# Output projection's norm and operand split moved into the heads' steps, meta tokens left out of the dense stages

## Chip, cores and metric

One NeuronCore of one Trainium2 chip runs the program. The metric is device time in microseconds, median of the runs shown. TensorE (PE), VectorE (DVE), ScalarE (ACT), GpSimd (POOL) and SyncE (SP, which only issues transfers here) each work through a queue of their own in order, and wait for each other by semaphores.

## What is computed

One layer of a hybrid encoder on T = 1152 token columns: 48 columns of padding, 16 learned meta tokens, 1024 prompt tokens and 64 sample tokens. All dense products are in fp32 accuracy.

```
proj = rms_norm(x, norm1) @ w_in                 # 1024 -> 2560 columns
o_r  = rwkv7_time_mix(proj[..., :1792], ...)     # 8 heads x 64, state recurrence, times the gate g
o_a  = window_attention(q, k, v, ...)            # 8 query heads, 2 kv heads, meta keys and sinks
o_a  = rms_norm(o_a, attn_out_norm)              # over the 512 columns of o_a
h    = x + concat(o_r, o_a) @ w_out              # 1024 -> 1024
u    = rms_norm(h, norm2) @ w_up                 # 1024 -> 4096
y    = h + square(relu(u)) @ w_down              # 4096 -> 1024
```

The outputs are y without the meta tokens, the new recurrent states, the last projected rows, and the attention's window and meta rows.

## The kernel before

Everything is kept with the features on the 128 partitions and the tokens along the row. A dense product splits both operands into an upper part rounded to fp32r and the rest, and adds three fp32r products (`three_pass`, L98 to L102: hi x hi, hi x lo, lo x hi). The tokens of a dense product come in three groups of columns (`GROUPS`, L25): 336, 384 and 384, each with a PSUM bank of its own.

`phase_project` makes the buffer `proj` (20 units of 128 features x 1152 columns): units 0 to 3 are r, 4 to 7 k, 8 to 11 v, 12 and 13 the low-rank inputs, 14 to 17 q, 18 and 19 the attention's k and v.

`phase_heads` (`loop_heads`, L630) goes through nine steps j of 128 tokens. Each engine has its own hand-written order of small functions (`step`), and PSUM banks go from use to use by a written list (`SCHEDULE`, L586; class `Fills` turns it into semaphore counts). A step inverts a 64 x 64 triangular system in five levels: PE multiplies (`product(j, l)`), DVE masks (`product`, L1259, the tile `Pm`), PE multiplies twice (`extend(j, l)`), ACT copies both results (`extended`, the tiles `X` and `XT`). Between the levels lie the attention of step j, the preparation (`prep_...`) of step j+1 and the output (`out_mean`, `out_var`, `out_gate`, `finish`) of step j-1. The attention's result is written over q in `proj` (`attended`, L1081) and the mixer's over r (`finish`, L1298, its last line L1308). On ACT `prep_rn` (L1032) makes the rstd of the keys in two passes, for which `prep_kkn` (L1188) waits on DVE; behind it in DVE's queue is the mask of level 4. POOL's `prep_rk` (L1408) waits for `prep_kkn`'s first line, `normed` (L1461) for ACT's `rstd`.

After the last step a barrier ends the phase (`end_phase`). `phase_block` then runs `mix_heads` (L1507): squares of o_a on ACT, their sums on DVE and through PE, the rstd on ACT, the scaling on DVE (L1558), and the split of all eight units into the new buffers `mix_hi` and `mix_lo`, upper parts on ACT, lower parts on DVE and, for three units of r, on POOL (L1569). Meanwhile SP fetches the first two column blocks of `w_out` (`out_fetch`, L1578, three transfers per block). `project_out` (L1642) then splits each block of `w_out` on ACT (L1684) and DVE (L1700), multiplies, adds x by a product with the identity (L1729), and starts the second norm; `mlp` (L1744) runs 16 blocks of 256 hidden units: `up` (48 matmuls for each of three groups of columns), ACT's relu, square and rounding, DVE's lower part (`hidden`), and `down` (48 per group), which DVE adds to h (`add`, L1918, L1923). In DVE's queue the adds of a block stand behind `up_weights` (L1900), the split of the next weights but one, which in turn waits for ACT's `up_weights` (L1849). A `down` matmul group with index 6 or more waits for the add six before it, since there are six banks.

Of the kernel before, what the change touches and what calls it, by code (L numbers as in the profile page):

```python
# [48 lines left out]
def build_program(nc, i, o):  # L49

    with ExitStack() as whole:
# [31 lines left out]
        def col(name, t=0, n=1):  # L83
# [4 lines left out]
                 w_stage=w_stage, bank=bank, col=col, bias=bias,  # L88
# [6 lines left out]
        phase_block(nc, i, o, s, projected.close)  # L95
# [360 lines left out]
def phase_heads(nc, i, o, s):  # L456
# [3 lines left out]
    with ExitStack() as ctx:  # L460
# [24 lines left out]

        kst = buf("kst", [P, 2, 144])
# [10 lines left out]
class Setup:  # L497
# [72 lines left out]
    def tensor(self, pe):  # L570
# [8 lines left out]
        for p in range(4):  # L579
# [50 lines left out]
def loop_heads(nc, s, v, setup, i, o):  # L630
# [19 lines left out]
        sem(n, 2) for n in "mx_ok nm_ok sk_ok se_ok pexp_ok den_ok rec_ok p_ok".split())  # L650
    hp_t, hp_c, cache_v = (sem(n) for n in "hp_t hp_c cache_v".split())
# [24 lines left out]
    AR = lambda j: AR2[:, j % 2]  # L676
    LAST = NT - 1

    with nc.Block() as block:
        @block.tensor  # L680
        def _(pe):
# [223 lines left out]
            def step(j):  # L905
# [73 lines left out]
            out_mean(LAST)  # L979
            out_var(LAST)  # L980
# [14 lines left out]
        def _(act):  # L995
# [112 lines left out]
            def step(j):  # L1108
# [52 lines left out]
            states = [proj[0:64, 9 + n, 0:512] for n in range(2)]  # L1161
            for n, dst in enumerate(states):
                act.activation(dst, bank[1 - n][0:64, :], ACT.Copy).then_inc(hp_c.sem, 1)
            for n, (src, name) in enumerate(zip(states, ("wkv_p", "wkv_s"))):
                act.wait_ge(hp_c.sem, hp_c.n(n))
                act.dma_start(o[name].rearrange("a b h v k -> v (a b h) k"), src.rearrange("v (h k) -> v h k", h=8)).then_inc(s["wkv_out"].sem, 16)

        @block.vector
        def _(dve):
# [139 lines left out]

            def transfers(j):  # L1310
# [165 lines left out]

# [28 lines left out]


def mix_heads(nc, i, s, v):  # L1507

    sem, proj, eps, bank, col, ones = (s[k] for k in "sem proj eps bank col ones".split())
    x_hi, x_lo = v["x_hi"], v["x_lo"]  # L1510
    s["wo_in"] = [sem(f"wo_loaded{b}", 48) for b in range(2)]
    sq_ok, added, sum_ok, ln_ok, rs_ok, scaled, hi_r, hi_a = (
        sem(f"mix_{n}") for n in "sq added sum ln rs scaled hi_r hi_a".split())

    def heads(t, c=PAD, n=T - PAD):

        return proj[:, t if t < 4 else 10 + t, c:c + n]

    with nc.Block() as block:
        @block.sync  # L1520
        def _(sp):
            for m in range(2):
                out_fetch(sp, i, s, m)
            sp.wait_ge(s["wkv_out"].sem, 32)

        @block.scalar
        def _(act):
            for t in range(4):
                act.activation(proj[:, 4 + t, PAD:T], heads(4 + t), ACT.Square).then_inc(sq_ok.sem, 1)
            for t in range(4):  # L1530
                act.activation(x_hi[:, t, PAD:T], heads(t), ACT.Copy).then_inc(hi_r.sem, 1)
            for g, (c, n) in enumerate(GROUPS):
                rs = proj[:, 8, c:c + n]
                act.wait_ge(sum_ok.sem, sum_ok.n(g))
                act.activation(rs, bank[g][:, 0:n], ACT.Ln, bias=eps[:, 0:1], scale=1.0 / 512).then_inc(ln_ok.sem, 1)
                act.wait_ge(ln_ok.sem, ln_ok.n(g))
                act.activation(rs, rs, ACT.Exp, scale=-0.5).then_inc(rs_ok.sem, 1)
            for g, (c, n) in enumerate(GROUPS):
                for t in range(4):
                    act.wait_ge(scaled.sem, scaled.n(4 * g + t))  # L1540
                    act.activation(x_hi[:, 4 + t, c:c + n], heads(4 + t, c, n), ACT.Copy).then_inc(hi_a.sem, 1)

        @block.vector
        def _(dve):

            for k, t in enumerate((1, 2, 3)):
                dve.wait_ge(sq_ok.sem, sq_ok.n(t))
                if k > 0:
                    dve.wait_ge(added.sem, added.n(k - 1))
                dve.tensor_tensor(proj[:, 4, PAD:T], proj[:, 4, PAD:T], proj[:, 4 + t, PAD:T], ALU.add).then_inc(added.sem, 1)  # L1550
            for t in range(3, 4):
                dve.wait_ge(hi_r.sem, hi_r.n(t))
                dve.tensor_tensor(x_lo[:, t, PAD:T], heads(t), x_hi[:, t, PAD:T].bitcast(F32), ALU.subtract)
            for g, (c, n) in enumerate(GROUPS):
                dve.wait_ge(rs_ok.sem, rs_ok.n(g))
                for t in range(4):
                    a = heads(4 + t, c, n)
                    dve.scalar_tensor_tensor(out=a, in0=a, scalar=col("an", t), in1=proj[:, 8, c:c + n],  # L1558
                                             op0=ALU.mult, op1=ALU.mult).then_inc(scaled.sem, 1)
                for t in range(4):  # L1560
                    dve.wait_ge(hi_a.sem, hi_a.n(4 * g + t))
                    dve.tensor_tensor(x_lo[:, 4 + t, c:c + n], heads(4 + t, c, n), x_hi[:, 4 + t, c:c + n].bitcast(F32),
                                      ALU.subtract)

        @block.gpsimd
        def _(pool):
# [541 lines left out]
```

## Time and profile before

| | us |
|---|---|
| median of 3 runs | 1687.83 (1686.51 to 1688.15) |
| the profiled execution: its time / its span | 1689.05 / 1687.0 |
| PE busy, share of the span | 1564.6, 93% |
| DVE / ACT / POOL busy | 777.4 / 579.6 / 125.4 |
| projection (start of the span to about) | 297 |
| nine steps of the heads, POOL's first `Tr` to its last: eight steps | 316.6 to 668.0 |
| last instruction of the heads on DVE, first matmul of the output projection | 719.65, 749.73 |
| output projection and MLP | 749.73 to 1687.0 |

A span is counted from the first instruction of the execution to the last. Busy time of an engine counts only its own instructions; how far it sets the time is seen from what the others wait for. The ends of matmuls are modelled, so the price of one matmul is read from the distance of two starts and not from its duration. An arrow in brackets at the end of a line gives the idle time of that engine before the instruction and who ended it. "us to landing" is counted from the issue of a transfer.

### The profile page before, as it was taken

What the parts mean: (1) busy time and instruction counts of PE and PEld (TensorE: products, weight loads), DVE (VectorE), ACT (ScalarE), POOL (GpSimd) and SP (SyncE); (2) the same over time, 40 slices, a digit from 0 to 9 for tenths busy, and PEclk for the clock granted to TensorE, in tenths of its full rate; (3) what the DMA queues carried; (4) which work ended last, traced back from release to release, by engine and by line L of the source; (5) the groups of instructions that cost most, each with busy time, mean ns of one, the idle gap of its engine ahead of it and who ended that gap; (6) DMA issues with size and microseconds to landing.
All of it is one profiled execution on the core that took longest, in us unless ns stands there. A gap on an engine that the chain in (4) does not pass through costs nothing. (4 is left out here: it accounts for less than half of the span.)

```text
span 1687.0 us, 37211 instructions
## 1 busy us (share of the span) xinstructions
PE 1564.6 (93%) x15821; PEld 1471.5 (87%) x15821; DVE 777.4 (46%) x1310; ACT 579.6 (34%) x1126; POOL 125.4 (7%) x131
## 2 busy tenths in 40 slices
PE   6999998689899998839999999999999999999998
PEld 6999997477777777629988999999999999999998
DVE  5123332567677766362233443333444333344444
ACT  6443211455555555452124222332222233322211
POOL 3000000222222222020000000000000000000000
PEclk9999998799999999959999999999999999999999
DMA  6111111000000000034002111101111111011003
GB/s 177 38 48 39 49 37 33 7 4 3 3 3 3 3 3 3 4 94 126 25 12 89 48 28 51 51 27 47 50 50 36 39 50 50 25 50 50 25 1 106
DMA packets 82531, 66.82 MB, mean 40 GB/s; under 512 B 14929, under 2 KB 74507, under 8 KB 82411
## 3 DMA queue, kind: packets, MB, share of 16 engines
q1 hardware_dynamic: 79939, 64.26, 12.9%
q8 instruction: 97, 1.59, 0.4%
q10 hardware_dynamic: 2408, 0.76, 0.2%
q14 instruction: 23, 0.19, 0.0%
q0 software_dynamic: 64, 0.03, 0.0%
HBM read 59.66 MB, written 5.44 MB: 39 GB/s over the span
## 5 line engine op out<-in xcount | busy, mean ns | idle before, releaser
L100 PE MATMUL bank<-mix_hi,uw_hi 128*128 128x384 f32 (+1 forms) x768 | 255.7, 333 | 6.6 <-DVE uw_lo L1903 6.6
L100 PE MATMUL bank<-u_hi,dw_hi 128*128 128x384 f32 (+1 forms) x768 | 255.5, 333 | 3.6 <-DVE dw_lo L1908 3.6
L1923 DVE TENSOR_TENSOR hT<-hT,bank 128x384 f32<-128x384 f32 (+1 forms) x384 | 197.3, 536 | 131.7 <-PE bank L102 131.7
L101 PE MATMUL bank<-mix_lo,uw_hi 128*128 128x384 f32 (+1 forms) x768 | 255.1, 332 | 0.0
L102 PE MATMUL bank<-mix_hi,uw_lo 128*128 128x384 f32 (+1 forms) x768 | 255.0, 332 | 0.0
L101 PE MATMUL bank<-u_lo,dw_hi 128*128 128x384 f32 (+1 forms) x768 | 253.7, 330 | 0.0
L102 PE MATMUL bank<-u_hi,dw_lo 128*128 128x384 f32 (+1 forms) x768 | 253.6, 330 | 0.0
L1915 DVE TENSOR_TENSOR u_lo<-xn,u_hi 128x384 fp32r<-128x384 f32 (+1 forms) x96 | 52.0, 542 | 308.8 <-ACT u_hi L1874 308.8
L100 PE MATMUL bank<-x_hi,w_hi 128*128 128x384 f32 (+1 forms) x480 | 160.2, 334 | 0.1
L101 PE MATMUL bank<-x_lo,w_hi 128*128 128x384 f32 (+1 forms) x480 | 158.4, 330 | 0.0
L102 PE MATMUL bank<-x_hi,w_lo 128*128 128x384 f32 (+1 forms) x480 | 158.3, 330 | 0.0
L100 PEld LDWEIGHTS bank<-mix_hi,uw_hi 128*128 128x128 f32 x768 | 145.4, 189 | 7.5 <-DVE uw_lo L1903 7.5
L100 PEld LDWEIGHTS bank<-u_hi,dw_hi 128*128 128x128 f32 x768 | 145.1, 189 | 5.7 <-DVE dw_lo L1908 3.9
L101 PEld LDWEIGHTS bank<-mix_lo,uw_hi 128*128 128x128 f32 x768 | 145.8, 190 | 0.0
L102 PEld LDWEIGHTS bank<-mix_hi,uw_lo 128*128 128x128 f32 x768 | 145.8, 190 | 0.0
L101 PEld LDWEIGHTS bank<-u_lo,dw_hi 128*128 128x128 f32 x768 | 145.2, 189 | 0.0
L102 PEld LDWEIGHTS bank<-u_hi,dw_lo 128*128 128x128 f32 x768 | 145.2, 189 | 0.0
L1856 ACT ACTIVATE dw_hi<-d_stage 128x1024 fp32r<-128x1024 f32 x32 | 32.1, 1051 | 313.0 <-PE bank L102 313.0
L1866 ACT ACTIVATE sq<-bank 128x384 f32<-128x384 f32 (+1 forms) x96 | 45.8, 477 | 224.0 <-PE bank L102 223.4
L100 PEld LDWEIGHTS bank<-x_hi,w_hi 128*128 128x128 f32 x480 | 90.5, 189 | 1.0 <-DVE x_lo L327 0.4
L101 PEld LDWEIGHTS bank<-x_lo,w_hi 128*128 128x128 f32 x480 | 90.4, 188 | 0.7
L102 PEld LDWEIGHTS bank<-x_hi,w_lo 128*128 128x128 f32 x480 | 90.4, 188 | 0.0
(272 smaller groups left out, 2476.2 us busy)
## 6 DMA issues: line engine op xcount, KB each, us to landing
w_stage<-in_w_up SPq DMA_DIRECT2D x32, 512.0 KB, 4.5
d_stage<-in_w_down SPq DMA_DIRECT2D x32, 512.0 KB, 4.2
w_stage<-in_w_in SPq DMA_DIRECT2D x16, 512.0 KB, 3.9
proj<-in_x SPq DMA_DIRECT2D x9, 512.0 KB, 5.1
xs<-in_x SPq DMA_DIRECT2D x9, 512.0 KB, 4.5
w_stage<-in_w_in SPq DMA_DIRECT2D x8, 256.0 KB, 4.3
w_stage<-in_w_out SPq DMA_DIRECT2D x8, 256.0 KB, 3.1
w_stage<-in_w_out SPq DMA_DIRECT2D x16, 128.0 KB, 4.0
```

Source lines behind the costliest of these rows:

```text
L100: pe.matmul(out, hi, x_hi, start=first, stop=False)
L101: pe.matmul(out, hi, x_lo, start=False, stop=False)
L102: return pe.matmul(out, lo, x_hi, start=False, stop=last)
L1856: act.activation(dw_hi[:, h], d_stage[:, h], ACT.Copy).then_inc(dwh.sem, 1)
L1866: act.activation(relu[:, e, 0:n], bank[k][:, 0:n], ACT.Relu).then_inc(up_read.sem, 1)
L1915: dve.tensor_tensor(u_lo[:, q, h, c:c + n], u32[:, e, 0:n], u_hi[:, q, h, c:c + n].bitcast(F32), ALU.subtract).then_inc(u_lo_ok.sem, 1)
L1923: dve.tensor_tensor(hT[:, m, c:c + n], hT[:, m, c:c + n], bank[j % 6][:, 0:n], ALU.add).then_inc(dn_add.sem, 1)
```

## The change

- The buffer `split` (fp32r) is laid over `proj`. The upper parts of r go over units 4 to 7 and those of o_a over 8 to 11; the lower parts go in place over units 0 to 3 and 14 to 17. `mix_hi`, `mix_lo`, `xs`, `d_stage` and (in the MLP) the hidden layer's scratch are no longer buffers of their own; four spare units of `proj` hold the last three.
- `mix_heads` is gone. In step j of the heads ACT makes the squares of o_a of step j-1 (`out_square`), PE sums them (`out_squares`, four matmuls with the matrix of ones between `prep_kk` and `extend(j, 3)`, PSUM bank 5), ACT makes the rstd of 128 columns (`out_rstd`, behind `extended(j, 3)` and ahead of `prep_rn`), DVE scales (`out_scale`, four instructions between `prep_kkn` and the mask of level 4), ACT rounds (`upper_a` for j-1, `upper_r` for j-2) and POOL subtracts (`lower_r` for j-2 behind `prep_rk`, `lower_a` for j-1 at the end of its step). What is left of the last two steps follows after the loop.
- The fetches of the first two blocks of `w_out` now stand at the head of `project_out`, ahead of the loads of x, and the wait for the states' store behind them.
- The first group of columns of the output projection and the MLP begins after the meta tokens (`TAIL_GROUPS`): 320 columns and not 336.

```diff
+M0 = PAD + N_META
+TAIL_GROUPS = [(M0, 384 - M0), (384, 384), (768, 384)]
...
         proj = sb("proj", [P, NU, T], F32, projected)
+        projected.close()
+        split = sb("split", [P, NU, T], F32R)
...
-            ("mean", 4, -1), ("p3", 0, 0), ("kk", 6, 1), ("e3", 1, 0), ("t3", 2, 0), ("pt0", 7, 0), ("pm0", 3, 0), ("p4", 0, 0),
+            ("mean", 4, -1), ("p3", 0, 0), ("kk", 6, 1), ("osum", 5, -1), ("e3", 1, 0), ("t3", 2, 0), ("pt0", 7, 0), ("pm0", 3, 0), ("p4", 0, 0),
...
+            def out_squares(j):
+                pe.wait_ge(osq_ok.sem, osq_ok.n(j))
+                f.await_room(pe, "osum", j)
+                for p in range(4):
+                    mm = pe.matmul(f.bank("osum")[:, 0:P], s["ones"][:], osq[:, P * p:P * p + P], start=p == 0, stop=p == 3)
+                mm.then_inc(f.full("osum"), 1)
...
                     prep_kk(j + 1)
+                if j > 0:
+                    out_squares(j - 1)
                 extend(j, 3)
...
+            def out_square(j):
+                f.await_read(act, "o0", j)
+                f.await_read(act, "o1", j)
+                if j > 0:
+                    f.await_full(act, "osum", j - 1)
+                act.activation(q4(osq[:]), o_in(j), ACT.Square).then_inc(osq_ok.sem, 1)
+
+            def out_rstd(j):
+                f.await_full(act, "osum", j)
+                if j > 0:
+                    act.wait_ge(o_ok.sem, o_ok.n(j - 1))
+                act.activation(ors[:], f.bank("osum")[:, 0:P], ACT.Ln, bias=eps[:, 0:1], scale=1.0 / 512).then_inc(f.read("osum"), 1)
+                f.await_read(act, "osum", j)
+                act.activation(ors[:], ors[:], ACT.Exp, scale=-0.5).then_inc(ors_ok.sem, 1)
+
+            def upper_a(j):
+
+                act.wait_ge(o_ok.sem, o_ok.n(j))
+                act.activation(split[:, 8:12, cols(j)], o_in(j), ACT.Copy).then_inc(hia_ok.sem, 1)
+
+            def upper_r(j):
+                f.await_read(act, "gate", j)
+                act.activation(split[:, 4:8, cols(j)], r_in(j), ACT.Copy).then_inc(hir_ok.sem, 1)
...
                 values_turned(j)
+                if j > 0:
+                    out_square(j - 1)
...
                     squares(j - 1)
+                if j > 1:
+                    upper_r(j - 2)
                 extended(j, 3)
+                if j > 0:
+                    out_rstd(j - 1)
...
                     rstd(j - 1)
+                    upper_a(j - 1)
                 probs(j, 1)
...
+            out_square(LAST)
             squares(LAST)
+            out_rstd(LAST)
             rstd(LAST)
+            upper_a(LAST)
+            upper_r(LAST - 1)
...
+            upper_r(LAST)
...
+            def out_scale(j):
+                dve.wait_ge(ors_ok.sem, ors_ok.n(j))
+                for p in range(4):
+                    a = proj[:, 14 + p, cols(j)]
+                    last = dve.scalar_tensor_tensor(out=a, in0=a, scalar=col("an", p), in1=ors[:], op0=ALU.mult, op1=ALU.mult)
+                last.then_inc(o_ok.sem, 1)
...
                     prep_kkn(j + 1)
+                if j > 0:
+                    out_scale(j - 1)
                 product(j, 4)
...
+            def lower_a(j):
+
+                pool.wait_ge(hia_ok.sem, hia_ok.n(j))
+                pool.tensor_tensor(split[:, 14:18, cols(j)], o_in(j), split[:, 8:12, cols(j)].bitcast(F32), ALU.subtract)
+
+            def lower_r(j):
+                pool.wait_ge(hir_ok.sem, hir_ok.n(j))
+                pool.tensor_tensor(split[:, 0:4, cols(j)], r_in(j), split[:, 4:8, cols(j)].bitcast(F32), ALU.subtract)
...
                     prep_rk(j + 1)
+                if j > 1:
+                    lower_r(j - 2)
                 if j > 0:
                     normed(j - 1)
                 if j < LAST:
                     prep_hat(j + 1)
                     keys(j + 1)
+                if j > 0:
+                    lower_a(j - 1)
...
+            lower_a(LAST)
+            lower_r(LAST - 1)
+            lower_r(LAST)
...
+HI, LO, SPARE = (4, 5, 6, 7, 8, 9, 10, 11), (0, 1, 2, 3, 14, 15, 16, 17), (13, 18, 19, 12)
...
-        v = dict(x_hi=sb("mix_hi", [P, KT, T], F32R, ctx, "right"),
-                 x_lo=sb("mix_lo", [P, KT, T], F32R, ctx, "right"))
-        mix_heads(nc, i, s, v)
-        free_proj()
...
+        v = dict(x_hi=lambda k, c, n: split[:, HI[k], c:c + n],
+                 x_lo=lambda k, c, n: split[:, LO[k], c:c + n],
+                 hT=sb("hT", [P, KT, T], F32, ctx), rs=sb("rs", [P, 384], F32, ctx))
...
+                for m in range(2):
+                    out_fetch(sp, i, s, m)
                 for t in range(3):
                     load_x(t)
+                sp.wait_ge(s["wkv_out"].sem, 32)
...
```

The whole of `mix_heads` is removed, and `GROUPS` becomes `TAIL_GROUPS` in every function of `project_out` and `mlp`.

## Rows read from the trace of the kernel before

**Rows 1.** Busy time by stretch: length, then each engine's us (instructions), granted clock.
```profile
300.00:700.00 400.00, 353.17 (x8508) 285.58 (x8508) 270.57 (x495) 205.27 (x482) 95.66 (x97) 0.98 0.02 4
...
1000.00:1400.00 400.00, 400.00 (x2375) 398.99 (x2375) 167.74 (x284) 104.02 (x177) 0.00 (x0) 1.00 0.15 42
```
**Rows 2.** Timeline of PE, one MLP block: start, duration, line, out<-in, shape.
```profile
1083.90 0.32 PE L100 MATMUL bank<-u_hi,dw_hi 128*128 128x336 f32 x1
...
1089.52 0.42 PE L100 MATMUL bank<-u_hi,dw_hi 128*128 128x336 f32 x1
...
1099.81 0.33 PE L100 MATMUL bank<-u_hi,dw_hi 128*128 128x384 f32 x1
...
1108.13 0.31 PE L100 MATMUL bank<-mix_hi,uw_hi 128*128 128x336 f32 x1
...
1111.81 0.35 PE L100 MATMUL bank<-mix_hi,uw_hi 128*128 128x384 f32 x1
...
1120.27 0.32 PE L100 MATMUL bank<-mix_hi,uw_hi 128*128 128x336 f32 x1
```
**Rows 3.** Timelines of ACT and DVE, same MLP block, at the start of `down`.
```profile
1085.61 2.00 ACT L1849 ACTIVATE uw_hi<-w_stage 128x1024 fp32r<-128x1024 f32 x2
...
1086.69 2.36 DVE L1903 TENSOR_TENSOR uw_lo<-w_stage,uw_hi 128x1024 fp32r<-128x1024 f32 x2 [0.40 <-ACT uw_hi L1849]
1088.96 3.40 DVE L1923 TENSOR_TENSOR hT<-hT,bank 128x336 f32<-128x336 f32 x8
```
**Rows 4.** Timelines from the heads' end to the output projection: DVE, SP, ACT, PE.
```profile
718.96 0.69 DVE L1308 TENSOR_TENSOR proj<-ys,bank 128x512 f32<-128x512 f32 x1
...
721.09 4.62 SPq L1584 DMA_DIRECT2D w_stage<-in_w_out  x6
...
747.36 2.00 ACT L1684 ACTIVATE wo_hi<-w_stage 128x1024 fp32r<-128x1024 f32 x2 [1.60 <-PEq L1519]
...
749.73 0.65 PE L100 MATMUL bank<-mix_hi,wo_hi 128*128 128x336 f32 x1 [18.19 <-DVE wo_lo L1700]
```
**Rows 5.** The page's issues of transfers: count, KB each, median us to landing.
```profile
w_stage<-in_w_out SPq DMA_DIRECT2D x16, 128.0 KB, 4.0
```
**Rows 6.** Timeline of PE, one step of the heads (j = 3, 449 to 493 us).
```profile
464.15 1.15 PE L726 MATMUL bank<-Pm,XT 64*64 64x64 f32 x32
...
467.53 0.66 PE L771 MATMUL bank<-ident,Lg 128*128 128x128 f32 x4 [1.30 <-DVE Lg L1291]
...
471.18 1.15 PE L726 MATMUL bank<-Pm,XT 64*64 64x64 f32 x32
...
477.45 1.16 PE L894 MATMUL bank<-proj,g2s 128*128 128x128 f32 x8
```
**Rows 7.** Timeline of ACT: the same step, and one 128-column pass in the last step.
```profile
467.95 0.63 ACT L1036 ACTIVATE SQ<-SQ 128x512 f32<-128x512 f32 x1
...
676.82 0.28 ACT L1054 ACTIVATE vtk<-bank 128x128 f32<-128x128 f32 x1 [0.31 <-PE bank L750]
```
**Rows 8.** Timeline of DVE, the same step.
```profile
468.61 0.69 DVE L1192 TENSOR_TENSOR Z<-BB,SQ 128x512 f32<-128x512 f32 x1 [1.13 <-ACT SQ L1036]
...
469.82 0.69 DVE L1256 TENSOR_TENSOR Pm<-bank,lvl 128x512 f32<-128x512 f32 x1
...
476.97 1.01 DVE L1287 TENSOR_TENSOR sm<-sm,sk 128x4 f32<-128x4 f32 x1
...
480.72 1.11 DVE L1302 TENSOR_SCALAR ys<-ys,par 128x128 f32<-128x128 f32 x4
```
**Rows 9.** Timeline of POOL, the same step.
```profile
469.38 1.42 POOL L1410 TENSOR_TENSOR SQ<-proj,par 128x512 f32<-128x512 f32 x1 [2.93 <-DVE Z L1192]
475.23 1.27 POOL L1463 TENSOR_TENSOR ys<-ys,yq 128x512 f32<-128x512 f32 x1 [4.43 <-ACT yq L1092]
476.46 1.50 POOL L1420 TENSOR_TENSOR bh<-Bt,L 128x512 f32<-128x512 f32 x1
```
**Rows 10.** Lines L1558 and L1569 of `mix_heads`: duration ns min/median/max, first and last start.
```profile
L1558 DVE SCALAR_TENSOR_TENSOR proj<-proj,par x12: 554/606/2815, 730.9 to 744.6; 128x384 f32<-128x384 f32 x8, 128x336 f32<-128x336 f32 x4
...
L1569 POOL TENSOR_TENSOR mix_lo<-proj,mix_hi x3: 2767/3450/3573, 726.4 to 733.3; 128x1104 fp32r<-128x1104 f32 x3
```

More of the change, by code:

```diff
@@ L87, in build_program @@
         s = dict(sem=sem, sb=sb, proj=proj, ident=ident, ones=ones, ones_bd=ones_bd, par=par, eps=eps, last_p=last_p,
-                 w_stage=w_stage, bank=bank, col=col, bias=bias,
+                 w_stage=w_stage, split=split, bank=bank, col=col, bias=bias,
                  wkv_out=Count(nc.alloc_semaphore("wkv_out")),
@@ L650, in loop_heads @@
         sem(n, 2) for n in "mx_ok nm_ok sk_ok se_ok pexp_ok den_ok rec_ok p_ok".split())
+    osq, ors, split = v["osq"], v["ors"], s["split"]
+    osq_ok, ors_ok, o_ok, hia_ok, hir_ok, mixed_ok = (sem(n) for n in "osq_ok ors_ok o_ok hia_ok hir_ok mixed_ok".split())
     hp_t, hp_c, cache_v = (sem(n) for n in "hp_t hp_c cache_v".split())
@@ L676, in loop_heads @@
     AR = lambda j: AR2[:, j % 2]
+    o_in = lambda j: proj[:, 14:18, cols(j)]
     LAST = NT - 1
@@ L979, in _ @@
             out_mean(LAST)
+            out_squares(LAST)
             out_var(LAST)
@@ L1157, in _ @@
                 step(j)
+            out_square(LAST)
             squares(LAST)
+            out_rstd(LAST)
             rstd(LAST)
+            upper_a(LAST)
+            upper_r(LAST - 1)
             act.wait_ge(hp_t.sem, hp_t.n(0))
-            states = [proj[0:64, 9 + n, 0:512] for n in range(2)]
+            states = [proj[0:64, 12, 512 * n:512 * n + 512] for n in range(2)]
             for n, dst in enumerate(states):
@@ L1398, in _ @@
             centre(LAST)
+            out_scale(LAST)
             finish(LAST)
@@ L1504, in phase_block @@
         mlp(nc, i, o, s, v)
[L1507 to L1566, printed above, removed]
-            for t in range(3):
-                pool.wait_ge(hi_r.sem, hi_r.n(t))
-                pool.tensor_tensor(x_lo[:, t, PAD:T], heads(t), x_hi[:, t, PAD:T].bitcast(F32), ALU.subtract)
-        @block.tensor
-        def _(pe):
-            pe.wait_ge(added.sem, added.n(2))
-            for g, (c, n) in enumerate(GROUPS):
-                pe.matmul(bank[g][:, 0:n], ones[:], proj[:, 4, c:c + n], start=True, stop=True).then_inc(sum_ok.sem, 1)
@@ L1651, in project_out @@
     xs_in = [sem(f"xs_loaded{b}") for b in range(XS)]
+    s["wo_in"] = [sem(f"wo_loaded{b}", 48) for b in range(2)]
     s["up_in"] = [sem(f"up_loaded{b}", 16) for b in range(2)]
@@ L1657, in project_out @@
         wo_lo = sb("wo_lo", [P, KT, KT, P], F32R, ctx)
-        xs = sb("xs", [P, XS, D_MODEL], F32, ctx)
+        xs = [s["proj"][:, u, 0:D_MODEL] for u in SPARE]
+        v.update(sq=sb("sq", [P, 2, 384], F32, ctx), xn=sb("xn", [P, 2, 384], F32, ctx))
         with nc.Block() as block:
@@ L1727, in _ @@
                             pe.wait_ge(xs_in[t % XS].sem, 16 * (t // XS + 1))
-                        lo = PAD if t == 0 else 0
-                        mm = pe.matmul(out[:, P * t + lo - c:P * t + P - c], xs[:, t % XS, P * m:P * m + P],
+                        lo = M0 if t == 0 else 0
+                        mm = pe.matmul(out[:, P * t + lo - c:P * t + P - c], xs[t % XS][:, P * m:P * m + P],
                                        ident[:, lo:P], start=False, stop=t == 3 * g + 2)
@@ L1762, in mlp @@
         u_hi, u_lo = (sb(f"u_{n}", [P, 2, 2, T], F32R, ctx) for n in ("hi", "lo"))
-        d_stage = sb("d_stage", [P, 2, D_MODEL], F32, ctx)
-        relu, u32 = v["sq"], v["xn"]
-        y_tok = [d_stage[:, 0], d_stage[:, 1], w_stage[:, 0].rearrange("p k c -> p (k c)"),
+        d_stage = [s["proj"][:, u, 0:D_MODEL] for u in SPARE[0:2]]
+        relu, u32 = (s["proj"][:, u, 0:768].rearrange("p (e n) -> p e n", e=2) for u in SPARE[2:4])
+        v["xn"] = u32
+        y_tok = [d_stage[0], d_stage[1], w_stage[:, 0].rearrange("p k c -> p (k c)"),
                  w_stage[:, 1].rearrange("p k c -> p (k c)")]
@@ L1855, in down_weights @@
                             act.wait_ge(dn_full.sem, dn_full.n(b - 1, 23))
-                        act.activation(dw_hi[:, h], d_stage[:, h], ACT.Copy).then_inc(dwh.sem, 1)
+                        act.activation(dw_hi[:, h], d_stage[h], ACT.Copy).then_inc(dwh.sem, 1)
                 def hidden(b, q):
```

53 lines of the change are left out of this document (26 added, 27 removed).

## The prediction

> **What bounds the kernel now.** I read busy time by stretch first, to see where PE is the limit. In the MLP it is busy 400.00 of 400 us with everything else under half; in the heads PE has 353 of 400 and DVE 271 [rows 1], so there PE is nearly full but each step also hangs on waits. Then the timeline of PE in one MLP block: matmuls start at fixed distances, so what a column costs can be read there [rows 2], and one matmul in the first group of `down` takes 0.42 where its neighbours take 0.32, because it waits for DVE's first add, whose time ACT's and DVE's weight split sets [rows 3]. Third, the passage from the heads to the output projection: DVE's last instruction ends at 719.65, the first matmul starts at 749.73 [rows 4]; those 30 us hold `mix_heads`, and ahead of the projection lie a fetch and a split of `w_out` [rows 4, 5]. Last, one step of the heads engine by engine [rows 6 to 9]: which instruction PE waits for, and what stands ahead of it in the queues.
>
> **Dense stages, 16 columns fewer.** In `up` 24 matmuls of 336 columns take from 1108.13 to 1111.81, 153.3 ns each; in `down` 48 of 384 take from 1099.81 to 1108.13, 173.3 each [rows 2]. That is 20 ns for 48 columns, so 16 columns are 6.7 ns. The first group has 768 matmuls in `up` and 192 in the output projection: 960 x 6.7 = 6.4 us. In `down` PE does not keep all of it: the 37th matmul waits for the add that begins at 1088.96, and the add stands behind the weight split, which began with ACT at 1085.61 [rows 3], counted from the end of `up`. None of that gets shorter, so what the first 36 save becomes waiting. The first 36 run at (1089.52 - 1083.90)/36 = 156.1 ns; against 146.7 the last 12 of 48 save 0.11 us a block, 16 blocks 1.8 us. (Without that wait it would be 768 x 9.4 ns = 7.2 us.) Eight identity products and eight norm sums lose 16 columns in fp32: 0.4 us, an estimate.
>
> There is a second gain which isn't in the columns. 384 columns cost 173.3 ns out of `u_hi` but (1120.27 - 1111.81)/48 = 176.3 out of `mix_hi` [rows 2]: same shape, same clock, another buffer. `mix_hi` lies at the right end of the memory, `u_hi` and `proj` are allocated from the left, and `split` takes `proj`'s place. I take 173.3 for it: 1536 + 384 matmuls x 2.9 ns = 5.6 us. Bounds: nothing, if the reason is not the place, and 5.6. Together **-14.2 us**, bounds -6.8 (columns only, nothing from `down`) and -19.6.
>
> The Trainium skill (TensorE: Matmul & The Clock Gate, section "Wait — 56ns, not 53.3ns?") gives a warm matmul as its columns at 2.4 GHz plus about 2.5 ns, the same for all. By it the place would bring nothing and the dense stages -8.1 (6.4 + 1.3 + 0.4). The rows differ: over the columns' own time they show 13 to 16 ns, and not the same from two buffers, so the sum goes by the rows.
>
> **The passage.** `finish(LAST)` still ends at about 719.65 (its chain through PE, ACT and POOL only gets four matmuls on PE, in a stretch where PE waits for ACT). Behind it come one rounding on ACT (0.63, [rows 7]) and one subtraction on POOL (1.27, [rows 9]): 721.7 with two handovers. From DVE's end to SP's first issue went 1.44 us [rows 4], so the fetch starts at 723.15. Six issues take 4.62 [rows 4]; the third starts 1.54 after the first and lands 4.0 later [rows 5], so block 0 is there after 5.5 us. ACT and DVE split it in 2.37 (747.36 to 749.73, [rows 4]). First matmul at 731.0 and not 749.73: **-18.7 us**. The loads of x now queue behind the fetches, but are needed only at the end of the first product. Bounds: 4.0 for the fetch (the landing alone) or 7.9 (block 0 there only with the last of the six), so -20.2 to -16.3.
>
> **The heads' steps.** Take step j = 3 and follow the new work.
> - PE: `out_squares` has the shapes of the gate's four matmuls, 1.16 us [rows 6], about 1.0 when the next work overlaps its end. `extend(3)` starts at 465.2 and not 464.15. PE itself loses nothing, since it idles 1.30 us ahead of 467.53 [rows 6], where it waits for DVE; without that idle time it would be 1.0 a step.
> - ACT: its copies come 1.0 later, then two passes of 128 columns, 0.28 each [rows 7], 0.5 in sequence. The last pass of `prep_rn` (467.95, [rows 7]) ends at 470.1 and not 468.6: 1.5 later. `out_square` and `upper_r` (0.63 each) lie where ACT waits for PE's transposes and for the later `extend(3)`. `upper_a` stands ahead of the second softmax, but DVE's sum behind that (476.97, 1.01 long for four elements) waits for POOL's `bh` until 477.96 anyway [rows 8, 9]. If that cover were gone, 0.5 a step.
> - DVE already waits 1.13 for `prep_rn` [rows 8], so `prep_kkn` moves by all of the 1.5, to 470.1. The keys' second product takes it to 471.35; there `out_scale` starts: four instructions, as long as those at 480.72 (1.11 in all, [rows 8]), 1.04 in sequence.
> - POOL: `prep_rk` is released by `prep_kkn` too, so it starts at 470.9 and ends at 472.3 (1.42, [rows 9]); `lower_r` follows without a wait, 1.27 as its like [rows 9], to 473.5. So both run beside `out_scale`. What that costs, `mix_heads` shows: this very instruction took 554 ns alone and 2815 beside POOL's subtractions, of 2767 at least [rows 10]: it waits until POOL's is over, and one gets through between two of POOL's. So the first of the four ends at about 472.45, the second at 473.65, the fourth at 474.1.
> - The mask of level 4, 469.82 to 470.51 [rows 8], moves to 474.1 to 474.8. PE's `extend(4)`, at 471.18 [rows 6], waits for it: **3.6 us** later (0.67 of it were slack). After it PE's rows follow each other without a wait up to the gate's end at 478.61, ACT and DVE take their times from them, and POOL's from ACT: nothing absorbs it.
>
> Bounds of that 3.6: 1.9, if POOL and DVE don't hold each other up (1.5 + 1.04 - 0.67), and 5.4 (third rival). I take 3.6, since row 10 is the same instruction beside the same work. Steps 2 to 7 pay 3.6, step 1 has no `lower_r` and pays 2.7, the last has neither `prep_rn` nor `prep_rk` and pays 1, for `upper_a` and `lower_a` ahead of the second softmax; `lower_a` at the end of POOL's step mostly lies in a wait of DVE, 1 us in all. 21.6 + 2.7 + 1 + 1 = **+26.3 us**, bounds 15.3 and 37.5.
>
> **Sum:** -14.2 - 18.7 + 26.3 = -6.6. The profiled execution took 1689.05 (span 1687.0 and 2 us around it), which gives 1682.5; it is 1.2 above the median of the runs shown, so I say **1681.2**.
>
> **Rivals.**
> 1. POOL and DVE don't meet, because the 128-column instructions slip through or `lower_r` comes earlier. Heads 1.9 x 7 + 2 = 15.3, sum -17.6: 1670.2. Against it stand rows 10, and the sum of four elements that took 1.01 us beside `bh` [rows 8, 9]; for it, that the second product of the keys isn't slowed beside `prep_rk`. The Trainium skill (SBUF — State Buffer, section "SBUF: two separate sides") says of that: a GpSimd instruction and a VectorE one with two SBUF inputs share a port pair, the first to start holds it for the whole instruction and the other blocks. By it this rival falls; the trace agrees with the 2815 ns.
> 2. The place of the operand brings nothing, nor does `down`: -6.8 - 18.7 + 26.3 = +0.8, 1688.6.
> 3. Slower: DVE becomes the chain through the whole step. Then all that stands in its queue or holds it up counts: 1.5 + 1.04 + 1.0 (`prep_rk`) + 1.27 (`lower_r`) + 1.27 (`lower_a`, which delays the masks and state updates that end the step) - 0.67 = 5.4 a step; 6 x 5.4 + 4.1 + 1 = 37.5, sum +4.6: 1692.4. It decides from about 4.7 us a step, 32.9 over seven. For it: DVE has only a third of idle time in the heads [rows 1]. Against it: that DVE idles ahead of the state products.
> 4. That the change doesn't do what it says (the norm still in a block of its own) the diff excludes.
>
> **How the numbers follow.** Forecast 0.50 (own range 1675 to 1688), rival 1 0.22, rival 2 0.13, rival 3 0.15. 0.2%, 3.4 us, is about what a measurement of this kernel can tell from no change. Faster by more: 0.37 of the forecast's 0.50, all of rival 1, 0.02 of rival 2: 0.61. Slower: 0.12 of rival 3 and 0.04 from forecast and rival 2: 0.16. The rest, 0.23, within. Range 1668 to 1692: it takes in rival 1 and reaches rival 3's value; steps dearer than 5.4 or a dense gain near 19.6 with cheap steps lie outside.
>
> **What would show it.** The first matmul of the output projection about 11 us later than `finish(LAST)`; `up` with 146.7 and 173.3 ns; at the 37th `down` matmul a wait of about 0.4 and not 0.1; the heads' steps 47.5 us long and not 43.9, with PE waiting for DVE's mask of level 4 ahead of `extend(4)`, and `out_scale` over 2 us long. The forecast is wrong if `out_scale` takes 1.1, or if steps lengthen at another place than `extend(4)`.

## The result, and the profile after

The changed kernel takes 1696.58 us in the median (1693.43 to 1702.51, five runs), the kernel before 1687.83 (1686.51 to 1688.25): a ratio of 1.0059, 95% interval 1.0040 to 1.0078. It is slower by about 9 us where 6.6 faster was forecast, and the time lies outside the range of 1668 to 1692. The profiled execution of the changed kernel took 1693.43 (span 1691.6), 4.4 above that of before, while the medians lie 8.75 apart: it was the fastest of its five. The parts below are cut on those two traces.

POOL's `diagonal` begins once in each step of the heads, so its starts cut the time into steps. First the kernel before, then the changed one: the starts of j = 0, 3, 4 and 8.

```profile
316.56 1.05 POOL L1446 TENSOR_TENSOR Tr<-id,elc 128x512 f32<-128x512 f32 x1
...
447.53 1.05 POOL L1446 TENSOR_TENSOR Tr<-id,elc 128x512 f32<-128x512 f32 x1 [4.07 <-PE bank L849]
...
491.83 1.05 POOL L1446 TENSOR_TENSOR Tr<-id,elc 128x512 f32<-128x512 f32 x1 [3.91 <-PE bank L849]
...
667.97 1.05 POOL L1446 TENSOR_TENSOR Tr<-id,elc 128x512 f32<-128x512 f32 x1 [3.69 <-PE bank L849]
```
```profile
316.95 1.05 POOL L1513 TENSOR_TENSOR Tr<-id,elc 128x512 f32<-128x512 f32 x1
...
454.97 1.05 POOL L1513 TENSOR_TENSOR Tr<-id,elc 128x512 f32<-128x512 f32 x1 [3.39 <-PE bank L860]
...
504.97 1.05 POOL L1513 TENSOR_TENSOR Tr<-id,elc 128x512 f32<-128x512 f32 x1 [3.47 <-PE bank L860]
...
703.83 1.05 POOL L1513 TENSOR_TENSOR Tr<-id,elc 128x512 f32<-128x512 f32 x1 [3.77 <-PE bank L860]
```

Eight steps take 351.4 us before and 386.9 after: **+35.5** (a second trace of the changed kernel, after_again in experiment 4, has 389.5). The step j = 3 took 44.3 and takes 50.0.

The passage, on the timelines of DVE, SP and PE of the changed kernel (answer to [rows 4]):

```profile
756.22 0.69 DVE L1365 TENSOR_TENSOR proj<-ys,bank 128x512 f32<-128x512 f32 x1
...
760.40 4.09 SPq L1598 DMA_DIRECT2D w_stage<-in_w_out  x6
...
767.15 0.64 PE L105 MATMUL bank<-split,wo_hi 128*128 128x320 f32 x1 [15.78 <-DVE wo_lo L1719]
```

From the start of `diagonal` of the last step to the first matmul of the output projection it was 749.73 - 667.97 = 81.8 us and is 767.15 - 703.83 = 63.3: **-18.4**. From that matmul to the end of the span it was 937.3 and is 924.4: **-12.8**. The three make +4.3 of the 4.4. The dense stages scatter: the nine traces of the changed kernel and of its edits that leave these stages alone have 923.8 to 929.1, the three of the kernel before and its edits 937.3 to 937.9, so the gain lies between 8 and 14 us.

One MLP block on PE's timeline (answer to [rows 2]):

```profile
1084.93 0.31 PE L105 MATMUL bank<-split,uw_hi 128*128 128x320 f32 x1
...
1088.44 0.34 PE L105 MATMUL bank<-split,uw_hi 128*128 128x384 f32 x1
...
1096.79 0.31 PE L105 MATMUL bank<-u_hi,dw_hi 128*128 128x320 f32 x1
...
1102.39 0.42 PE L105 MATMUL bank<-u_hi,dw_hi 128*128 128x320 f32 x1 [0.17 <-DVE hT L1943]
...
1120.92 0.31 PE L105 MATMUL bank<-split,uw_hi 128*128 128x320 f32 x1
```

24 matmuls of 320 columns out of `split` take 3.51 us, 146.3 ns each; 48 of 384 take 8.35, 174.0 each (176.3 out of `mix_hi`). The 37th matmul of `down` waits for DVE's first add; the 36 ahead of it take 155.6 ns each with that wait, as long as the 156.1 of before.

The step j = 3 on PE, then on DVE and POOL (answer to [rows 6, 8, 9]):

```profile
482.31 1.97 PE L737 MATMUL bank<-Pm,XT 64*64 64x64 f32 x32 [3.63 <-DVE Pm L1313]
...
484.07 1.61 PE L737 MATMUL bank<-XT,Pm 64*64 64x64 f32 x32
...
492.30 0.66 PE L782 MATMUL bank<-ident,Lg 128*128 128x128 f32 x4 [0.92 <-DVE Lg L1348]
...
497.19 0.69 PE L835 MATMUL bank<-w_stage,WU 64*64 64x64 f32 x32 [1.04 <-DVE proj L1365]
```
```profile
478.74 2.92 DVE L1371 SCALAR_TENSOR_TENSOR proj<-proj,par,ors 128x128 f32<-128x128 f32 x4
481.58 0.68 DVE L1313 TENSOR_TENSOR Pm<-bank,lvl 128x512 f32<-128x512 f32 x1
...
494.50 1.65 DVE L1362 TENSOR_TENSOR ys<-ys,proj 128x512 f32<-128x512 f32 x1
```
```profile
478.30 1.42 POOL L1477 TENSOR_TENSOR SQ<-proj,par 128x512 f32<-128x512 f32 x1 [4.42 <-DVE Z L1249]
479.68 1.30 POOL L1539 TENSOR_TENSOR split<-proj,split 128x512 fp32r<-128x512 f32 x1
...
494.33 1.28 POOL L1535 TENSOR_TENSOR split<-proj,split 128x512 fp32r<-128x512 f32 x1
```

Counted from the step's start, `extend(4)` was at 471.18 - 447.53 = 23.65 and is at 27.34: 3.7 later, as forecast, by the mechanism forecast (`out_scale` 2.92 long between `prep_rk` and `lower_r`, the mask of level 4 behind it). But its batch takes 1.97 us and not 1.15, and the next 1.61; at the second `turn_probs` the step is 492.30 - 454.97 - (479.65 - 447.53) = 5.2 late and at its end 5.7. The windows of steps 1 to 7 as a whole and of this stretch show what came in (length; busy time of PE, weight loads, DVE, ACT and POOL with their instructions; the granted clock, as a share of 2.4 GHz; DMA share and GB/s):

```profile
357.00:704.00 347.00, 299.48 (x6938) 243.19 (x6938) 238.19 (x428) 178.88 (x413) 91.44 (x92) 0.96 0.01 3
480.00:486.00 6.00, 3.69 (x68) 3.43 (x68) 5.88 (x12) 0.86 (x2) 0.99 (x1) 0.72 0.01 3
```
```profile
357.00:704.00 347.00, 315.63 (x7661) 254.39 (x7661) 234.60 (x435) 181.85 (x424) 78.73 (x80) 1.00 0.01 3
```

The second fence is the kernel before, 1.00 over the same 347 us. Behind the wait for the mask TensorE is granted 1.2 GHz instead of 2.4 for some microseconds; the 0.72 is the mean of the 6 us.

### The profile page after: what moved, and what is told of

Read it like the earlier page. It is cut to its first block and busy times, and to the rows that moved or that the text cites. A ratio compares the mean times of both kernels' runs of the same rounds, so it can differ in the third digit from the quotient of the medians.

```text
span 1691.6 us, 37397 instructions
## 1 busy us (share of the span) xinstructions
PE 1559.3 (92%) x15887; PEld 1466.6 (87%) x15887; DVE 776.7 (46%) x1318; ACT 579.8 (34%) x1145; POOL 137.1 (8%) x146
## 3 DMA queue, kind: packets, MB, share of 16 engines
q8 instruction: 98, 1.61, 0.4%
## 5 line engine op out<-in xcount | busy, mean ns | idle before, releaser
L105 PE MATMUL bank<-split,uw_hi 128*128 128x384 f32 (+1 forms) x768 | 251.6, 328 | 6.6 <-DVE uw_lo L1923 6.6
L107 PE MATMUL bank<-split,uw_lo 128*128 128x384 f32 (+1 forms) x768 | 251.4, 327 | 0.0
L106 PE MATMUL bank<-split,uw_hi 128*128 128x384 f32 (+1 forms) x768 | 251.3, 327 | 0.0
L1935 DVE TENSOR_TENSOR u_lo<-proj,u_hi 128x384 fp32r<-128x384 f32 (+1 forms) x96 | 51.5, 537 | 299.7 <-ACT u_hi L1894 299.7
L105 PEld LDWEIGHTS bank<-split,uw_hi 128*128 128x128 f32 x768 | 145.1, 189 | 7.5 <-DVE uw_lo L1923 7.5
L106 PEld LDWEIGHTS bank<-split,uw_hi 128*128 128x128 f32 x768 | 145.1, 189 | 0.0
L107 PEld LDWEIGHTS bank<-split,uw_lo 128*128 128x128 f32 x768 | 145.0, 189 | 0.0
L1876 ACT ACTIVATE dw_hi<-proj 128x1024 fp32r<-128x1024 f32 x32 | 32.2, 1053 | 311.0 <-PE bank L107 311.0
L1886 ACT ACTIVATE proj<-bank 128x384 f32<-128x384 f32 (+1 forms) x96 | 45.5, 473 | 215.7 <-PE bank L107 215.1
```

Source lines behind the costliest of these rows:

```text
L105: pe.matmul(out, hi, x_hi, start=first, stop=False)
L106: pe.matmul(out, hi, x_lo, start=False, stop=False)
L107: return pe.matmul(out, lo, x_hi, start=False, stop=last)
L1876: act.activation(dw_hi[:, h], d_stage[h], ACT.Copy).then_inc(dwh.sem, 1)
L1886: act.activation(relu[:, e, 0:n], bank[k][:, 0:n], ACT.Relu).then_inc(up_read.sem, 1)
L1935: dve.tensor_tensor(u_lo[:, q, h, c:c + n], u32[:, e, 0:n], u_hi[:, q, h, c:c + n].bitcast(F32), ALU.subtract).then_inc(u_lo_ok.sem, 1)
```

## Experiments

All are edits of the changed kernel, but for two of the kernel before. Ratios are to the kernel before, on the same chip.

**1. `out_scale` later (scale_late).**
```diff
 DVE    prep_kkn(j + 1)
-       out_scale(j - 1)
        product(j, 4)
        prep_bb, logits(j, 1), prep_bt(j + 1)
+       out_scale(j - 1)
        product(j, 5)
 ACT    upper_a(j - 1): from ahead of probs(j, 1) to behind attended(j, 0)
```


> The changed kernel with one thing moved: out_scale stands on DVE behind prep_bt (ahead of the mask of level 5), no longer ahead of the mask of level 4, and upper_a on ACT follows behind the first copies of the values (attended(j, 0)). Same instructions, another order. Theory A (the step pays at one place: PE's wait for the mask of level 4, and TensorE's clock, granted at half after that wait): the mask follows the second product of the keys and starts 2.8 us earlier in the step, PE waits about 0.8 instead of 3.6 us ahead of extend(4), the granted clock stays at 1.00 there and the two batches of extend(4) take about 1.15 us each instead of 1.97 and 1.61; 4.2 us for each of steps 2 to 7 and 2 for step 1, some 27 in all: about 1669. If the clock has no part in it, only the wait goes: 18 us, about 1678. Theory B (third rival of the prediction: DVE is the chain through the whole step, so its queue's place does not matter): 1693 to 1698.

1689.64 us, 1.0015 (1.0001 to 1.0029): 7 us gained, not 27. PE and DVE of the step j = 3, from their timelines:

```profile
480.61 1.15 PE L737 MATMUL bank<-Pm,XT 64*64 64x64 f32 x32 [0.80 <-DVE Pm L1314]
...
481.32 1.75 DVE L1259 SCALAR_TENSOR_TENSOR KE<-KE,proj 128x512 f32<-128x512 f32 x1
...
484.82 1.12 DVE L1340 TENSOR_TENSOR sk<-nm,sink 128x4 f32<-128x4 f32 x1
...
486.47 1.94 DVE L1372 SCALAR_TENSOR_TENSOR proj<-proj,par,ors 128x128 f32<-128x128 f32 x4
...
489.06 1.29 PE L737 MATMUL bank<-XT,Pm 64*64 64x64 f32 x32 [3.20 <-DVE Pm L1314]
...
490.28 2.07 PE L905 MATMUL bank<-proj,g2s 128*128 128x128 f32 x8
```

The wait for the mask of level 4 went as expected (0.80), and a wait of 3.20 for the mask of level 5 took its place, with the clock down behind it. On DVE, `KE` was held by `lower_r` (1.75 us, 0.68 in the kernel before), a subtraction of four elements by `normed` (1.12, there 0.16), and `out_scale` by `bh`. So my theory A was too narrow: from the keys' second product to the mask of level 5 DVE has no room, and what stands there or holds it is paid at one mask or the other.

**2. PE kept busy in the wait (warm_wait).**
```diff
-pe.matmul(var, ones_bd, yq, start=True, stop=True).then_inc(...)
+for _ in range(4 if j < LAST else 1):
+    mm = pe.matmul(var, ones_bd, yq, start=True, stop=True)
+mm.then_inc(...)
```


> The changed kernel with more work on PE alone: the matmul of out_var is issued four times over instead of once (the same result), right ahead of the wait for the mask of level 4; three more of it, some 0.86 us each by the 512 columns in four passes, lie inside that wait of 3.6 us. Theory A (the wait lets the granted clock fall to half, and the work behind it pays): the granted clock stays near 1.00 in this stretch, extend(4) takes about 1.15 us for each batch, the step gets about 1.4 us shorter although PE has more to do: about 9 us less in all, 1687. Rival (the slower extend(4) has another cause, such as ACT's copies): the batches stay at 1.97 and 1.61, and the time at 1695 to 1700.

1689.67 us, 1.0008 (0.9999 to 1.0018): 7 us less, with more work on PE. The timeline of PE, same step:

```profile
476.76 3.70 PE L901 MATMUL bank<-yq,ones_bd 128*128 128x512 f32 x8
481.53 1.15 PE L737 MATMUL bank<-Pm,XT 64*64 64x64 f32 x32 [1.07 <-DVE Pm L1315]
482.51 1.10 PE L737 MATMUL bank<-XT,Pm 64*64 64x64 f32 x32
```

The mask comes when it came, `extend(4)` takes 1.15 and 1.10, and the clock is 1.00 over all the steps. That separates the clock from the wait. The 7 us are a net figure: the eight steps got 8.3 us shorter (386.9 to 378.6 on the traces), and the last step, which has no such wait to fill, pays 2.6 for the three matmuls (its `extend(4)` starts 24.65 behind the step's start and not 22.07). So of the 35.5 us some 8 are the clock's.

**3. POOL's two subtractions moved (lower_moved).**
```diff
 POOL   diagonal(j)
+       lower_r(j - 2); lower_a(j - 2)
        prep_lx(j + 1); prep_rk(j + 1)
-       lower_r(j - 2)
        normed(j - 1); prep_hat(j + 1); keys(j + 1)
-       lower_a(j - 1)
 ACT    upper_r(j - 2): from behind squares(j - 1) to behind the copy of tr_v
```


> The changed kernel with POOL's two subtractions moved: lower_r and lower_a of tile j-2 stand behind diagonal(j) at the start of POOL's step (upper_r behind the copy of the value tokens on ACT, which releases them in the stretch where DVE waits for PE), out_scale stays where it is. Theory A (POOL's subtractions hold DVE: lower_r lengthens out_scale from 1.1 to 2.9 us, lower_a lengthens the sum ahead of the gate from 0.69 to 1.65): out_scale meets prep_rk alone and ends about 1 us earlier, the gate's product about 1 us earlier, so about 2 us for each of steps 2 to 7: 1684. The clock still falls, as PE still waits more than 2 us for the mask. Rival (the lengths do not come from POOL, or the subtractions hold DVE as long at their new place): no change, 1694 to 1698.

1686.38 us, 0.9989 (0.9974 to 1.0003): 10 us less. `out_scale` takes 1.91, the sum ahead of the gate 0.69, PE waits 2.63 and not 3.63. DVE and PE, step j = 3:

```profile
478.64 1.91 DVE L1371 SCALAR_TENSOR_TENSOR proj<-proj,par,ors 128x128 f32<-128x128 f32 x4
...
481.20 1.15 PE L737 MATMUL bank<-Pm,XT 64*64 64x64 f32 x32 [2.63 <-DVE Pm L1313]
```

The hold by POOL is confirmed. One thing was missed: behind that wait the clock stayed at 1.00 in three of seven steps.

**4. `lower_a` alone, and `out_rstd` alone**, with the changed kernel again beside them (after_again: 1697.15 us, 1.0052, 1.0035 to 1.0069).
```diff
 POOL   lower_a(j - 1) at the step's end -> lower_a(j - 2) behind diagonal(j)   (lower_a_only)
 ACT    out_rstd(j - 1) from ahead of prep_enl to behind prep_rn                (rstd_only)
```


> The changed kernel as it is, on the chip of the two runs beside it: 1694 to 1700, with the granted clock at 0.96 to 0.97 over the heads' steps and PE's wait of 3.6 us ahead of extend(4).

> The changed kernel with lower_a alone moved: POOL does it for tile j-2 behind diagonal(j), at the start of the next step, where DVE waits for PE most of the time; lower_r, out_scale and the rest stay. In the changed kernel the sum ahead of the gate's product takes 1.65 us beside lower_a instead of 0.69, and a step of the profile is 5.2 us late at the second turn_probs and 5.7 at its end. If what follows from that is the price of lower_a: 0.5 us in each of seven steps, 3.5 us, 1693. The prediction's price (1 us in all): 1696. If all 0.96 us of the hold counts: 7 us, 1690. The mask of level 4 and the clock behind it stay as they are.

> The changed kernel with out_rstd alone moved, behind prep_rn on ACT: the last pass of prep_rn ends 0.65 us earlier, so the second product of the keys, prep_rk, lower_r, out_scale and the mask of level 4 come 0.65 earlier, and PE waits 3.0 us ahead of extend(4) instead of 3.6. If the granted clock still falls behind that wait: 0.65 x 7 = 4.5 us, 1692. If it stays at 1.00, as it did behind the wait of 2.63 us in lower_moved: another 1.4 in six steps, 1684.

`lower_a` alone: 1694.23 us, 1.0033 (1.0020 to 1.0045), 2.9 below the changed kernel beside it: 0.4 a step, about what the lateness at the step's end had said. The two intervals overlap, but the trace shows the way: the sum ahead of the gate's product is back at 0.69, and PE starts the state products (L835) at 500.04 without the wait of 1.04.

```profile
498.30 0.69 DVE L1362 TENSOR_TENSOR ys<-ys,proj 128x512 f32<-128x512 f32 x1
```

`out_rstd` alone: 1687.88, 0.9991 (0.9976 to 1.0006), between the two values expected, and single runs from 1680.8 to 1691.7. The trace shows a reason. Here are `extend(4)` of its steps 2 and 3, and the windows of 6 us from each:

```profile
432.26 1.97 PE L737 MATMUL bank<-Pm,XT 64*64 64x64 f32 x32 [2.73 <-DVE Pm L1313]
...
481.29 1.15 PE L737 MATMUL bank<-Pm,XT 64*64 64x64 f32 x32 [2.74 <-DVE Pm L1313]
```
```profile
432.26:438.26 6.00, 6.00 (x126) 5.16 (x128) 3.96 (x9) 3.19 (x7) 0.71 (x1) 0.77 0.01 3
481.29:487.29 6.00, 5.71 (x151) 4.74 (x153) 4.86 (x10) 4.43 (x14) 1.95 (x2) 1.00 0.02 4
```

The same work behind the same wait begins at half clock in one step and runs at full clock in the next. In this run the clock fell in three of seven steps; those are 49.05 to 49.38 us long, the others from step 2 on 47.18 to 47.95.

**5. Three moves at once (scale_lower_rstd):** those of 1, 3 and `out_rstd`.

> The changed kernel with three moves at once: out_scale ahead of the mask of level 5 (as in scale_late), lower_r and lower_a at the start of POOL's step (as in lower_moved), and out_rstd on ACT behind prep_rn. Theory A (only the mask of level 4 matters, and lower_a): nothing of the new work is left in the way but 0.2 us behind out_squares: steps of 44.3, about 1661. Theory A2 (DVE is the chain up to the mask of level 5): out_scale's 1.04 us, held up to 0.9 more by POOL's bh, and normed's hold of about 1 us, less 1.05 us of idle time, stay in the way, the mask of level 5 is about 2.5 us later in the step: steps of about 46.5, PE waiting some 2 us ahead of extend(5), about 1677.

1676.56 us, 0.9931 (0.9914 to 0.9947): theory A2's value. `out_scale` takes 2.95 beside POOL's `normed` and `bh`, and PE waits at level 5:

```profile
481.43 2.95 DVE L1372 SCALAR_TENSOR_TENSOR proj<-proj,par,ors 128x128 f32<-128x128 f32 x4
...
485.03 1.15 PE L737 MATMUL bank<-XT,Pm 64*64 64x64 f32 x32 [2.25 <-DVE Pm L1314]
```

That the value was hit is in part luck. A2 gave steps of 46.5 us without a term for the clock. In the trace the granted clock is 0.96 in five of the steps 1 to 7, which take 46.9 to 47.4, and 1.00 in the other two, which take 45.2 and 45.6.

**6. The place alone, in the kernel before (before_dve_mid, before_dve_gap).**
```diff
+for p in range(4):      # j > 0, into a buffer that nobody reads
+    dve.scalar_tensor_tensor(out=junk[:, P*p:P*p+P], in0=ones, scalar=col("an", p), in1=ident, op0=mult, op1=mult)
 mid: ahead of product(j, 4)      gap: behind the copy of ktok
```


> The kernel before with four more instructions on DVE in each step but the first, of out_scale's form (128 columns, two operands in SBUF), on constants and into a buffer that nobody reads, ahead of the mask of level 4: the place that the change gave out_scale, with nothing else of the change. Theory A2: the first of them waits for the end of POOL's prep_rk (started 0.44 us earlier, 1.42 long), the four take about 2.0 us, less 0.67 of slack: 1.3 us a step in eight steps, about 10 us more, 1698; the wait of PE stays under 2 us and the granted clock at 1.00. Without a hold by prep_rk: 0.4 a step, 1691. If the place had enough slack: 1688.

> The kernel before with the same four instructions of DVE on constants behind the copy of the key tokens, where DVE waits 2.63 us for PE. Theory A2 (the start of the step is free): no change, 1687 to 1689. If DVE were the chain through the whole step: 1.04 us in each of eight steps, 1696 to 1697.

1697.78 us, 1.0063 (1.0048 to 1.0078), and 1690.00, 1.0006 (0.9992 to 1.0019): the same four instructions cost 10 us at the one place and nothing that can be told from no change at the other. Of the first, DVE, POOL and PE:

```profile
471.58 1.92 DVE L1357 SCALAR_TENSOR_TENSOR junk<-ones,par,ident 128x128 f32<-128x128 f32 x4
```
```profile
471.14 1.42 POOL L1415 TENSOR_TENSOR SQ<-proj,par 128x512 f32<-128x512 f32 x1 [2.92 <-DVE Z L1193]
```
```profile
474.15 1.15 PE L727 MATMUL bank<-Pm,XT 64*64 64x64 f32 x32 [1.14 <-DVE Pm L1257]
```

**7. The meta columns back (all_columns):** `TAIL_GROUPS = GROUPS`.

> The changed kernel with the column groups of the kernel before in the dense stages (the 16 meta columns are computed again: groups of 336, 384 and 384). The terms of the prediction: 6.4 us for up and the output projection, 1.8 in down and 0.4 for identity products and norm sums come back, +8.6 us: about 1705; matmuls of 384 columns out of split keep the 174 ns of the changed kernel, and the 37th matmul of down waits about 0.1 us again. Rival (the columns bring less, and most of the dense gain of 12.8 us is the operand's place): 1697 to 1700.

1709.16 us, 1.0126 (1.0105 to 1.0147), 12.6 above the changed kernel. From the first matmul of the output projection to the end it is 1705.6 - 770.09 = 935.5, 11.1 above the changed kernel's 924.4 where 8.6 was expected. Against the scatter of 923.8 to 929.1 that single difference decides little; the rows do. The rows of one unit of `up`:

```profile
1141.08 0.31 PE L105 MATMUL bank<-split,uw_hi 128*128 128x336 f32 x1
...
1144.82 0.34 PE L105 MATMUL bank<-split,uw_hi 128*128 128x384 f32 x1
...
1153.16 0.31 PE L105 MATMUL bank<-u_hi,dw_hi 128*128 128x336 f32 x1
```

336 columns out of `split` take 155.8 ns (153.3 out of `mix_hi`, [rows 2]) and 384 take 173.8. The new buffer is better for the one shape and worse for the other. So by rows the columns are worth 960 x (155.8 - 146.3) = 9.1, with 1.8 and 0.4 as forecast 11.3.

**8. All of it in the holes of a step (dve_gaps).**
```diff
 DVE    prep_kk0(j + 1)
+       out_scale(j - 2); lower_r(j - 2)
        logits(j, 0); product(j, 2); copy of ktok
+       lower_a(j - 2)
        centre(j - 1)
 PE     out_squares(j - 1): behind out_gate(j - 1), in bank 7
 ACT    out_square behind prep_exp, out_rstd behind attended(j, 0),
        upper_a(j - 2) behind the copy of tr_v, upper_r(j - 1) ahead of attended(j, 1)
-POOL   lower_a, lower_r
```


> The changed kernel with the same work laid into the holes of a step: out_scale(j-2) and lower_r(j-2) on DVE ahead of the first softmax (where DVE waits 2.23 us for PE), lower_a(j-2) on DVE behind the copy of the key tokens (2.63 us of waiting), no subtraction on POOL any more; out_squares on PE ahead of the second turn_probs, where PE waits for DVE; the square and the root on ACT where ACT waits for PE. Theory A2 (formed on the trace of scale_late: DVE is the chain from the second product of the keys to the mask of level 5, whatever stands there or holds it counts, and the start of the step is free): the steps come back to 44.0 to 44.5 us, no wait over 1.5 us on PE, granted clock 1.00 throughout the heads; the passage (18.4 us) and the dense stages (12.8 us) keep their gains: 1657 to 1662. If DVE were the chain through the whole step, the 2.3 us of new work on it would count in full: steps of 46.2, about 1674.

1658.76 us, 0.9820 (0.9807 to 0.9834): it beats both kernels. The two holes on DVE, step j = 3 of the kernel before:

```profile
456.28 0.82 DVE L1273 SCALAR_TENSOR_TENSOR Lg<-bank,bias 128x288 f32<-128x288 f32 x2 [2.23 <-PE bank L761]
...
462.12 0.69 DVE L1295 SCALAR_TENSOR_TENSOR ys<-bank,ys 128x512 f32<-128x512 f32 x1 [2.63 <-PE bank L884]
```

DVE of the step j = 3 in this run, and the window of steps 1 to 7:

```profile
453.61 1.13 DVE L1371 SCALAR_TENSOR_TENSOR proj<-proj,par,ors 128x128 f32<-128x128 f32 x4
454.66 0.69 DVE L1380 TENSOR_TENSOR split<-proj,split 128x512 fp32r<-128x512 f32 x1
455.92 0.82 DVE L1330 SCALAR_TENSOR_TENSOR Lg<-bank,bias 128x288 f32<-128x288 f32 x2 [0.58 <-PE bank L772]
...
459.49 0.69 DVE L1376 TENSOR_TENSOR split<-proj,split 128x512 fp32r<-128x512 f32 x1 [0.36 <-ACT split L1132]
```
```profile
357.00:704.00 347.00, 324.52 (x7760) 262.61 (x7764) 249.81 (x476) 199.22 (x463) 78.26 (x80) 1.00 0.01 3
```

`out_scale` is as long as alone, DVE still waits 0.58 for PE behind it, the clock is 1.00, and the eight steps take 667.06 - 317.30 = 349.8 us, no longer than the 351.4 of before (without the first step, which scatters, 308.8 and 309.1). The passage gains 19.6 us and the dense stages, at 928.3, 9.0 and not 12.8.

## Why the prediction was wrong

**Dense, -14.2: right in size.** -12.8 on the two traces. By rows: 960 x (153.3 - 146.3) = 6.7 for the columns of `up` and the output projection (6.4 said), 1920 x 2.3 = 4.4 for the place (5.6), and a `down` shorter by 24.23 - 24.13 = 0.10 a block, 1.6 (1.8). That `down` gives back its first 36 was right. The split into columns and place was not: in the new buffer 336 columns would have cost 2.5 ns more each, which experiment 7 shows, so the place gained less and the columns more.

**Passage, -18.7: right.** Cut from the last step's start on, the forecast is -17.7, with the 1 us that the heads' sum puts on that step; -18.4 was measured. The fetch is issued 3.5 us behind the end of `finish(LAST)`, as forecast, and the first matmul stands 10.2 behind it (11 said).

**Heads, +26.3: the step that failed.** Without the last step's 1 us the forecast for the eight steps is +25.3; +35.5 was measured. The size at `extend(4)` was right: 3.6 said, 3.7 measured, by the hold that the prediction took from [rows 10], though the instruction there has 384 columns and not 128. `out_scale` takes 2.92 us beside POOL's two instructions and 1.13 with POOL away (experiment 8). The Trainium skill (SBUF — State Buffer, section "SBUF: two separate sides") states that of a GpSimd instruction that reads SBUF and a VectorE one with two SBUF inputs the first to start holds a shared pair of ports for the whole instruction, and the other is blocked. The 2.92 agrees. What failed is the sentence after it in the prediction, that PE's rows follow each other without a wait behind the mask and the step is 3.6 longer. Two things are missing from it.
- The granted clock. I priced a wait of 3.6 us at its own length. Behind it TensorE runs at 1.2 GHz, `extend(4)` and what follows take some 1.4 us longer, in six of the seven steps of the profile. Experiment 2 takes this away and shortens the eight steps by 8.3 us.
- `lower_a`, 1 us in all, "mostly lies in a wait of DVE". It holds the sum ahead of the gate's product, which the state products wait for: 0.4 a step, 2.9 us in experiment 4.

With 3.7 + 1.4 + 0.5 a step of the profile is 5.6 longer; steps 2 to 7 came out 33.3 us longer in all where 21.6 stood in the sum, step 1 3.5 and not 2.7. The first step, in which nothing was added, was 1.3 shorter. That is scatter: it takes 42.4 us in the kernel before, 41.1 and 41.0 in that kernel's two edits, and 40.6 to 42.7 in the others.

The Trainium skill (TensorE: Matmul & The Clock Gate, section "HAM oscillation — how this bites in real kernels") describes a kernel in which PE's waits for transfers between stretches of matmuls let the clock fall, so that each stretch begins at the lower one. Here, with waits for DVE, the trace agrees in six of seven steps, and the prediction did not weigh it.

**The rivals.** The third gave 1692.4 and came nearest, at 5.4 a step. Half of its mechanism holds: DVE is the chain from the keys' second product to the mask of level 5 (experiments 1, 5, 6). As the chain through the whole step it falls: experiment 8 puts 2.3 us of new work on DVE, POOL's two subtractions among it, and costs nothing. The first rival falls with the 2.92; the second with the dense stages. The range missed because its slow end was rival 3's value, in which all that stands in DVE's queue counts, but nothing of what a wait does to PE's clock.

## What to carry to other kernels

Before work is moved into a step, list for each engine where it waits within the step and for whom: the same norm and split cost 35 us in front of PE's masks and nothing in two holes of 2.2 and 2.6 us on DVE. Work on POOL beside a loaded DVE can be paid on DVE, by an instruction that has nothing to do with it. Not every instruction was held: the mask of level 4, one of whose operands lies in PSUM, took its usual 0.68 beside `prep_rk` in experiment 1. And a new wait of some microseconds on PE is to be priced with the slower matmuls behind it, here 1.4 us behind a wait of 3.6, in six steps of seven.

## What was not expected of the hardware

The granted clock does not fall behind each wait of the same length. In seven steps of one run it fell in six (waits of 3.64 us but for the first, of 2.64, where it did not), in another in three (2.73, the first 1.73), in a third in four (all 2.63). In after_again it fell in all seven, behind a wait of 2.63 too. What decides in which steps was not found. In the ten runs of `out_rstd` alone the time follows the mean granted clock (1680.83 us at 0.983, 1691.73 at 0.973), so there the clock is the likely cause of the scatter. It does not explain the slowest run of the changed kernel, 1702.51 us at 0.970, beside 1693.43 at 0.971.

An instruction of DVE on four elements took 1.12 us beside POOL's `normed` and 0.16 otherwise: the hold does not scale with the work held.

What a matmul takes beyond its columns differs with the buffer that its operand lies in, and with opposite sign for 336 and 384 columns (+2.5 and -2.3 ns from `mix_hi` to `split`). The reason was not looked for.
